# The score matmuls of a head pair in another order: the 256-column ones of both heads first, then the 128-column ones

## The reference

```python
def forgetting_attention(q, k, v, cum_logf_h):
    ...
    for i in range(s // Q_BLOCK):           # 2 blocks of 128 queries
        q0 = i * Q_BLOCK
        end = q0 + Q_BLOCK
        q_b = q[:, q0:end]
        k_b = k[:, :end]                    # 128 keys for block 0, 256 for block 1
        sc = jnp.einsum('bqhd,bkhd->bhqk', q_b, k_b).astype(jnp.float32) * scale
        ...
        p = jax.nn.softmax(sc, axis=-1).astype(v.dtype)
        outs.append(jnp.einsum('bhqk,bkhd->bqhd', p, v_b))
```

## Time and profile before

| | |
|---|---|
| median of 3 runs | 2678.65 us |
| the runs | 2678.65, 2684.79, 2678.27 us |
| span of the profiled execution | 2676.1 us |
| TensorE matmuls busy | 2648.9 us, 99% |
| VectorE, ScalarE, GpSimd busy | 1830.3, 1355.1, 139.8 us |
| mean granted TensorE clock | 0.998 |
| loop pass of one head pair | 47.42 us |

### The profile page before, as it was taken

How to read it: one execution, slowest core, us unless ns; L and a number is a source line. 1 busy time by engine, 2 the same in 40 slices (tenths; PEclk the granted TensorE clock), 3 DMA queues, 4 the chain that set the end, 5 groups by cost and what they waited for, 6 DMA issues and landing times.

```text
span 2676.1 us, 45331 instructions
## 1 busy us (share of the span) xinstructions
PE 2648.9 (99%) x16733; PEld 2376.3 (89%) x16733; DVE 1830.3 (68%) x2740; ACT 1355.1 (51%) x2060; POOL 139.8 (5%) x141
## 2 busy tenths in 40 slices
PE   8999999999999999999999999999999999999998
PEld 7888888888888888888888888888999899999987
DVE  7666566665675576666666666765889996689976
ACT  6444444444454454444444444544574674465664
POOL 0100000000000000101011010000000000000000
PEclk9999999999999999999999999999999999999999
DMA  7666666676666656667666666665555665565663
GB/s 230 206 195 208 192 196 203 194 208 193 201 195 189 189 162 204 196 194 206 195 206 194 197 203 194 198 193 189 181 172 175 184 190 173 165 189 187 207 212 126
DMA packets 513658, 514.76 MB, mean 192 GB/s; under 512 B 26922, under 2 KB 502466, under 8 KB 513282
## 3 DMA queue, kind: packets, MB, share of 16 engines
q1 hardware_dynamic: 490260, 488.01, 59.7%
q10 hardware_dynamic: 23296, 25.36, 3.3%
HBM read 489.93 MB, written 21.53 MB: 191 GB/s over the span
## 4 chain that ended last, share of the span: by engine, by line
PE 84%; DVE 10%; ACT 4%; issue 2%; DMA 1%; ACTq 0%; SPq 0%; DVEq 0%
PE proj L1344 34%; PE proj L1346 17%; PE proj L1359 9%; PE proj L1361 4%; PE proj L1527 4%; PE proj L1528 4%; PE proj L1529 4%; DVE scratch L2323 2%; DVE w_both L2164 2%; PE proj L1721 2%; PE ps_s L1432 1%; PE ps_s L1418 1%; PE proj L1723 1%; ACT w_both L963 1%; ACT scratch L1104 1%
## 5 line engine op out<-in xcount | busy, mean ns | idle before, releaser
L1344 PE MATMUL proj<-operand,w_both 128*128 128x512 f32 x3968 | 1400.5, 398 | 1.3 <-issue 0.8
L1820 DVE TENSOR_TENSOR w_both<-w_raw,w_both 128x1024 fp32r<-128x1024 f32 x644 | 792.2, 1233 | 660.0 <-ACT w_both L738 659.0
L1346 PE MATMUL proj<-operand,w_both 128*128 128x256 f32 x4096 | 1143.3, 279 | 0.0
L738 ACT ACTIVATE w_both<-w_raw 128x1024 fp32r<-128x1024 f32 x644 | 678.3, 1058 | 862.6 <-PE proj L1346 656.2
L1344 PEld LDWEIGHTS proj<-operand,w_both 128*128 128x128 f32 x3968 | 744.9, 188 | 178.5 <-issue 1.2
L1346 PEld LDWEIGHTS proj<-operand,w_both 128*128 128x128 f32 x4096 | 772.1, 188 | 0.8
L1527 PE MATMUL proj<-operand,w_both 128*128 128x272 f32 (+2 forms) x1540 | 447.2, 290 | 5.2 <-DVE w_both L2164 4.8
L1528 PE MATMUL proj<-operand,w_both 128*128 128x272 f32 (+2 forms) x1540 | 442.4, 287 | 0.0
L1529 PE MATMUL proj<-operand,w_both 128*128 128x272 f32 (+2 forms) x1540 | 442.0, 287 | 0.0
L1359 PE MATMUL proj<-w_both,operand 128*128 128x512 f32 x1024 | 357.8, 395 | 0.0
L2164 DVE TENSOR_TENSOR w_both<-w_raw,w_both 128x1024 fp32r<-128x1024 f32 x226 | 274.2, 1218 | 112.7 <-ACT w_both L963 111.9
(11 more groups left out here) (363 smaller groups left out, 2021.8 us busy)
## 6 DMA issues: line engine op xcount, KB each, us to landing
w_raw<-in_a_w_in_dram SPq DMA_DIRECT2D x256, 512.0 KB, 3.7
w_raw<-in_w_in_dram SPq DMA_DIRECT2D x160, 512.0 KB, 3.8
w_raw<-in_b_w_in_dram SPq DMA_DIRECT2D x128, 512.0 KB, 3.8
w_raw<-in_kv_w_dram SPq DMA_DIRECT2D x128, 512.0 KB, 4.1
w_raw<-in_a_w_out_dram SPq DMA_DIRECT2D x64, 512.0 KB, 4.1
w_raw<-in_b_w_out_dram SPq DMA_DIRECT2D x64, 512.0 KB, 4.3
w_raw<-in_w_out_dram SPq DMA_DIRECT2D x64, 512.0 KB, 3.6
probabilities<-scratch ACTq DMA_DIRECT2D x32, 384.0 KB, 2.5
```

The source lines that it names most:

```text
L738: act.activation(w_hi[:, s], w_raw[:, s], ACT.Copy).then_inc(hi_ready, 1)
L1344: pe.matmul(proj[:, 2 * bank + t, :], w_hi[:, s, kk, cols], rhs[:, k, :], start=first and k == 0, stop=False)
L1346: m = pe.matmul(proj[:, 2 * bank + t, 0:S], w_lo[:, s, kk, cols], rhs[:, k, 0:S], start=False, stop=last and end)
L1820: dve.tensor_tensor(w_lo[:, s], w_raw[:, s], w_hi[:, s].bitcast(F32), ALU.subtract).then_inc(pieces_split, 1)
```

## The change

Within a head pair the loop over the two heads held a 128-column and a 256-column matmul. Now a first loop issues the 256-column matmul of each head and a second loop the 128-column matmul of each head. The matmuls, their operands and their places in PSUM are the same. `scores_done` still hangs on the last of the four.

```diff
@@ -1414,8 +1414,9 @@
                 pe.wait_ge(scaled, 3 * n + 2)
                 pe.wait_ge(og_done, n + 1)
                 for h in range(2):
-                    pe.matmul(ps_s[:, h, 0:P], q_t[:, h, 0:P], k_t[:, h, 0:P], start=True, stop=True)
-                    m = pe.matmul(ps_s[:, h, P:384], q_t[:, h, P:S], k_t[:, h, :], start=True, stop=True)
+                    pe.matmul(ps_s[:, h, P:384], q_t[:, h, P:S], k_t[:, h, :], start=True, stop=True)
+                for h in range(2):
+                    m = pe.matmul(ps_s[:, h, 0:P], q_t[:, h, 0:P], k_t[:, h, 0:P], start=True, stop=True)
                 m.then_inc(scores_done, 1)
                 multiply(unit + 3, 1, h_q)
 
```

## The result

The changed kernel takes 2687.16 us (median of 20 runs, 2680.05 to 2697.07), the kernel before 2680.59 us (median of 20 runs, 2676.61 to 2688.75). The ratio is 1.0023, 95% interval 1.0014 to 1.0033: slower by 0.23%, some 6 us, where I had forecast no change and a range that ends at 2681.3. The size is within the 0.3% I had called no change; the time lies outside the range. Of the 8.5 us between forecast and result, 1.9 are the kernel before itself, whose median over 20 runs is 2680.59 and not the 2678.65 of the three runs that I had. One slow run of the kernel before, 9253.84 us in the set beside e1 to e4, is left out of the ratios.

What follows compares the result with a forecast made beforehand. TensorE's matmul stream was taken as the bound. The score stretch's 0.86 + 0.22 + 0.45 = 1.53 us against 1.54 counted as zero, so span 2676.1 plus 2.5 us carried over gave 2678.7 us, range 2677.4 to 2681.3.

Steps and rivals of the forecast that it cites:

- What bounds the kernel: Whole kernel: TensorE's own matmul stream sets the end, busy 99% of the span and carrying 84% of the last-ending chain.
- The score stretch: First score record to L1346 in each head pair: 1.53 us after against 1.54 before, taken as zero change.
- Four short records in a row: The two 128-column score matmuls, now adjacent: records stay 0.11 us each; one uncovered weight load would cost 0.08 us a pair.
- long ones with a change of bank: 256-column score matmuls of different heads, changing PSUM bank and weights at once: no gap expected, 0.43 us each.
- Rival B: Score stretch: weight loads fall behind in the run of short matmuls, 7.7 us slower, or 18 us fully bare; chance 2%.
- A: Score stretch: rival in which both heads' matmuls overlap, saving 21 us, to 2657.9 us; chance 1%.
- The handover: From the last score record to VectorE's first read of the scores: costs nothing, with 1.8 us of cover.
- A change on that engine counts unless it leaves the stream as long as it was: TensorE's matmul stream: an edit there moves the end only if it alters the stream's length; here taken as zero.
- Case C: Score stretch: one weight load bare or saved, 0.01 to 0.08 us a pair, -1.3 to +2.6 us; chance 12%.

Runs made afterwards that it cites:

- e1: The kernel before, run again unchanged for its profile: 2682.84 us, ratio 0.9998 to the kernel before.
- e4: Against the kernel before, the new score order in phase B (second attention phase) alone, the old order kept in phase A: ratio 1.0011.
- e2: The changed kernel, run again unchanged: 2689.69 us, ratio 1.0019 to the kernel before.
- e12: The changed kernel, run a third time unchanged: 2684.67 us, ratio 1.0012 to the kernel before.

## Why the prediction was wrong

- What bounds the kernel: right. TensorE's stream sets the end, and the loss is in that stream.
- The score stretch, 1.53 against 1.54 us: right, it is 1.54 in both.
- Four short records in a row, and long ones with a change of bank: right, no weight load shows. Rival B did not come, nor A.
- The handover, 1.8 us of cover: right, VectorE idles before no read.
- "A change on that engine counts unless it leaves the stream as long as it was", with the sum made over 1.54 us a pair: this step failed. I summed the edited stretch and took the other 45.9 us of the pass as fixed. They are not: 128 couples a pass run at 346.7 or 353.3 ns, and how the scores cut the stream selects which. The term that is missing is 64 couples x 6.7 ns = 0.43 us (0.42 measured) for each pass that turns all slow, up to 15 passes a phase. Over the profiles at hand 54 of 120 pass lengths (8 phases) were all slow with the new order and 7 of 90 (6 phases) with the old. For 30 passes in two phases that would be 30 x (0.45 - 0.08) x 0.42 = 4.7 us, 0.17%; the three sets of runs gave 1.0023, 1.0019 and 1.0012.
- Case C, a shift of 0.01 to 0.08 us a pair, is no hit: it meant a weight load bare or saved in the score stretch, where nothing moved, and the loss of 0.42 us a pass is five times its upper end and stands elsewhere. That the change stayed within 0.3%, which I gave 96%, is luck in the same way: the reason given, a stream as long as before, doesn't hold, and e2's profiled execution is 0.7% longer than the first one of the kernel before. The profile before could have shown the term: passes of 47.42 us but also two of 47.00 and one of 47.79, and couples of 0.36 and of 0.35 us in the same line. I read the one pass I needed and not their spread.
- The range from 2677.4 to 2681.3 was made of the rounding of starts (1.3 us down) and one bare load a pair (2.6 us up); the spread of the executions was left out of it, though the three runs at hand already spread over 6.5 us. The medians of the kernel before itself ran from 2678.65 us (3 runs) to 2682.84 (e1).

Shown are the two patterns, that they account for phase A's loss in the profiled execution, that the step at which the stream is cut and the order of the scores decide what follows, and that with another projection stream the loss goes away. Open are three things. What in TensorE makes the patterns. How much of the loss is the newly closed step 1: of the all-slow passes with the new order, 22 stood in the cycle of step 1 (phase B of e2 and of e12), and 29 in that of step 2 (phase A of the first profile and of e2), which the old order leaves closed too. And the third, whether the old order falls into step 2 less often for a reason or by luck: 3 of its 96 score cuts were at step 2, against 29 of 128. The passes of a phase are not independent, so this counts few phases: 4 of 8 fell into a long all-slow cycle with the new order and none of 6 with the old. The runs are more: 17 of 41 of the changed kernel took over 2688 us (a bound chosen afterwards), against 8 of 131 of the kernel before, all sets taken together. So the difference is there, and the kernel before can be that long as well.

## What to carry to other kernels

On an engine that is busy all the time, the length of an edited stretch is not the cost of an edit: read the same repeated stretch in many passes, before and after, and price a spread between them as a term of its own. If a long stream shows two periods, try a stream in which one is left; here that gave 0.26% and took away the cost of the order. A change of 0.2% needs more than a dozen runs on either side and more than one profile, since each execution picks its own cycle: the set of 20 and 20 runs told it from none, the one of 12 and 17 (e12) didn't.

## What the runs showed of the hardware

A stream of couples of matmuls with 512 and 256 columns, all of 128 x 128 weights and at the level of 2.4 GHz, settled in one of two periods, 693 ns for two couples or 1060 ns for three, and kept it through a whole projection of 32 couples and the next one behind it, through semaphore waits that were already met, until matmuls of another kind or a stall cut it. Two matmuls of 512 columns followed by two of 256 took 1.40 us for four couples, in every steady pass. In the fp32 score products a 128-column matmul left two records 0.11 us apart, four such records in a row without a gap, and a 256-column one two records 0.22 us apart.
